# Gate and up projections of an expert pair, expert by expert instead of chunk by chunk, with one semaphore for each weight slot

## The reference, cut to what matters

```python
def expert_block(args):                    # for each expert e, over the tokens sent to it
    b_tok, b_w, e = args
    xb = xt[b_tok]
    h = jax.nn.silu(xb @ w_gate[e]) * (xb @ w_up[e])
    return (h @ w_down[e]) * b_w[:, None].astype(xt.dtype)
...
routed = jax.ops.segment_sum(y_rows.reshape(rows, d), row_tok, num_segments=t)
shared = (jax.nn.silu(xt @ sw_gate) * (xt @ sw_up)) @ sw_down
return (routed + shared).reshape(bsz, s, d)
```

## Time and profile before

| | |
|---|---|
| median of 3 runs | 1241.08 us |
| the profiled execution | 1241.98 us |
| its span (first to last instruction) | 1240.2 us |
| PE busy | 1183.7 us (95%), 7261 MATMUL records |
| PE weight loads busy | 546.2 us (44%) |
| DVE busy | 489.9 us (40%) |
| ACT busy | 193.6 us (16%) |
| read from HBM | 456.51 MB, 373 GB/s over the span |
| mean granted TensorE clock | 0.992 |

### The profile page before, as it was taken

The page is one execution under the profiler, slowest core; times in us unless marked ns, Lnnn a source line. Parts: engine busy times, 40 slices in busy tenths (PEclk is TensorE's granted clock), DMA queues, the critical chain, the costliest instruction groups (busy, mean ns, idle before and its releaser), DMA issues.

```text
span 1240.2 us, 17629 instructions
## 1 busy us (share of the span) xinstructions
PE 1183.7 (95%) x7261; PEld 546.2 (44%) x7261; DVE 489.9 (40%) x1059; ACT 193.6 (16%) x330; POOL 47.2 (4%) x78
## 2 busy tenths in 40 slices
PE   9999999999999999988899999999999999998886
PEld 8774833333333333332386757333333333333322
DVE  5895733332323332322237157333333232332224
ACT  3231311111111111110122313111111111111102
POOL 6300100000000000000010001000000000000000
PEclk9999999999999999999989999999999999999998
DMA  9788799999999999999953596999999999999995
GB/s 348 211 300 360 297 383 412 414 422 420 421 421 422 421 421 421 421 421 420 402 190 126 202 382 248 392 414 407 421 421 420 420 422 420 422 421 421 420 420 215
DMA packets 83642, 463.98 MB, mean 374 GB/s; under 512 B 9264, under 2 KB 10608, under 8 KB 38384
## 3 DMA queue, kind: packets, MB, share of 16 engines
q1 hardware_dynamic: 83424, 462.37, 92.2%
q10 hardware_dynamic: 144, 0.52, 0.1%
HBM read 456.51 MB, written 6.36 MB: 373 GB/s over the span
## 4 chain that ended last, share of the span: by engine, by line
PE 72%; DMA 22%; DVE 2%; SPq 1%; ACT 1%; issue 1%; DVEq 0%; POOL 0%; POOLq 0%
PE bank L1216 30%; DMA expert_weights<-in_exp_w_up 21%; PE bank L1272 12%; PE bank L724 5%; PE bank L738 4%; PE bank L1136 4%; PE bank L1166 3%; PE bank L812 2%; PE bank L1154 2%; DMA weight_ring<-in_sh_w_up 1%; PE bank L839 1%; PE bank L1085 1%; PE bank L828 1%; PE bank L1159 1%; PE bank L1232 1%; SPq L316 1%
## 5 line engine op out<-in xcount | busy, mean ns | idle before, releaser
L1216 PE MATMUL bank<-expert_weights,weight_ring 128*64 128x512 f32 x1024 | 226.8, 595 | 12.3 <-DMA expert_weights<-in_exp_w_up 12.3
L1272 PE MATMUL bank<-expert_weights,hiddenT 128*32 128x512 f32 x1888 | 218.4, 595 | 7.8 <-DVE hiddenT L2097 3.6
L2094 DVE TENSOR_TENSOR hidden<-silu_gate,bank 128x256 f32<-128x256 f32 x64 | 26.9, 421 | 391.7 <-ACT silu_gate L1492 391.7
L1216 PEld LDWEIGHTS bank<-expert_weights,weight_ring 128*64 128x64 f32 x1024 | 70.6, 137 | 166.6 <-issue 139.7
L1216 PE MATMUL bank<-expert_weights,hT 128*64 128x512 f32 x512 | 118.6, 606 | 17.2 <-DMA expert_weights<-in_exp_w_up 17.2
L1272 PEld LDWEIGHTS bank<-expert_weights,hiddenT 128*32 128x32 f32 x1888 | 56.4, 109 | 159.3 <-issue 138.9
L1216 PE MATMUL bank<-expert_weights,octet_high 128*64 128x512 f32 x512 | 115.3, 592 | 0.0
L2106 DVE TENSOR_SCALAR y_top<-bank,slot_gate 128x512 fp32r<-128x512 f32 x64 | 48.0, 750 | 126.2 <-PE bank L1272 126.2
L1492 ACT ACTIVATE silu_gate<-bank 128x256 f32<-128x256 f32 x64 | 24.7, 386 | 438.4 <-PE bank L1216 438.4
L1496 ACT ACTIVATE y_top<-bank,slot_gate 128x512 fp32r<-128x512 f32 x64 | 44.0, 687 | 286.4 <-PE bank L1272 286.4
L1216 PEld LDWEIGHTS bank<-expert_weights,hT 128*64 128x64 f32 x512 | 34.3, 138 | 101.4 <-issue 64.5
(11 more groups left out here) (388 smaller groups left out, 1114.2 us busy)
## 6 DMA issues: line engine op xcount, KB each, us to landing
expert_weights<-in_exp_w_down SPq DMA_DIRECT2D x114, 1024.0 KB, 17.2
expert_weights<-in_exp_w_gate SPq DMA_DIRECT2D x108, 1024.0 KB, 14.2
expert_weights<-in_exp_w_up SPq DMA_DIRECT2D x108, 1024.0 KB, 16.3
expert_weights<-in_exp_w_gate SPq DMA_DIRECT2D x40, 512.0 KB, 9.1
expert_weights<-in_exp_w_up SPq DMA_DIRECT2D x40, 512.0 KB, 10.9
weight_ring<-in_w_in_even SPq DMA_DIRECT2D x5, 2048.0 KB, 11.6
spare_down<-in_exp_w_down SPq DMA_DIRECT2D x10, 1024.0 KB, 11.8
weight_ring<-in_w_out SPq DMA_DIRECT2D x4, 2048.0 KB, 7.8
```

Of the source, the lines that this page charges most:

```text
L1216: last_mm = nc.tensor.matmul(bank[6][a * 2 * CAP:(a + 1) * 2 * CAP, :].rearrange("p (w f) -> p w f", w=2), octet_tokens(l, v, c)[:, 2 * q ...
L1272: last_mm = nc.tensor.matmul(bank[b][by_tile:by_tile + CAP, :], hm[:, j, own:own + CAP], down[a][:, j, half * 512:(half + 1) * 512], start ...
L2094: nc.vector.tensor_tensor(hslot[:, :], sg[:, :], bank[6][:, DE:2 * DE], ALU.mult)\
```

## The change

PE: the loop over the expert `a` becomes the outer one and the loop over the chunks `c` the inner one, so all 8 chunks of expert 0 come first, then all 8 of expert 1. Before each expert PE waits on a semaphore of that slot alone (`gu_in[2u+a]`, two loads). After expert 0 it raises a new semaphore `gu_first`. The waits and increments in the middle of a pair are gone. In the very first pair, the waits for each chunk of gathered tokens stand in expert 0's loop alone.

SP: gate and up of slot 2u are refilled on `gu_first`, those of slot 2u+1 on `gu_full`. `expert_chunks` and the loads by halves are gone; every load of gate and up is a whole one of 1 MB. The order of the down loads and of the spare buffers stays, and so do the halves of the last down loads. `early_refills` writes out the same sequence for the first pairs.

```diff
--- before.py
+++ after.py
@@ -204,11 +204,9 @@
                   "bt ct stored c_in b_in direct gla_ln gla_last decays masked hstat hstd yhead states y_s5 "
                   "gelu5 out_full")
         for l in range(2):
-            for name in ("gu_in", "d_in"):
-                MO[l][name] = [sem(f"moe{l}_{name}{u}") for u in range(2)]
-            MO[l]["second_part"] = sem(f"moe{l}_second_part")
-            MO[l]["last_part"] = sem(f"moe{l}_last_part")
-            MO[l]["gu_part"] = sem(f"moe{l}_gu_part")
+            MO[l]["gu_in"] = [sem(f"moe{l}_gu_in{s}") for s in range(NSLOT)]
+            MO[l]["d_in"] = [sem(f"moe{l}_d_in{u}") for u in range(2)]
+            MO[l]["gu_first"] = sem(f"moe{l}_gu_first")
             MO[l]["spare_in"] = sem(f"moe{l}_spare_in")
         ring_in = [sem(f"ring_in{i}") for i in range(2)]
 
@@ -313,16 +311,8 @@
         def expert_load(sp, m, l, e, s):
             src_g = A["exp_w_gate"][l, e].rearrange("(p c) f -> p (c f)", c=KC)
             src_u = A["exp_w_up"][l, e].rearrange("(p c) f -> p (c f)", c=KC)
-            sp.dma_start(ew[:, s, 0:EW], src_g).then_inc(m["gu_in"][s // 2], 16)
-            sp.dma_start(ew[:, s, EW:2 * EW], src_u).then_inc(m["gu_in"][s // 2], 16)
-
-        def expert_chunks(sp, l, e, s, chunks, landed):
-
-            lo, hi = chunks[0] * DE, (chunks[-1] + 1) * DE
-            src_g = A["exp_w_gate"][l, e].rearrange("(p c) f -> p (c f)", c=KC)
-            src_u = A["exp_w_up"][l, e].rearrange("(p c) f -> p (c f)", c=KC)
-            sp.dma_start(ew[:, s, lo:hi], src_g[:, lo:hi]).then_inc(landed, 16)
-            sp.dma_start(ew[:, s, EW + lo:EW + hi], src_u[:, lo:hi]).then_inc(landed, 16)
+            sp.dma_start(ew[:, s, 0:EW], src_g).then_inc(m["gu_in"][s], 16)
+            sp.dma_start(ew[:, s, EW:2 * EW], src_u).then_inc(m["gu_in"][s], 16)
 
         def down_half(sp, l, e, s, part, landed):
 
@@ -410,7 +400,6 @@
         def spare_load(sp, m, a, src):
             sp.dma_start(spare_d[a][:, :, :].rearrange("p j n -> p (j n)"), src).then_inc(m["spare_in"], 16)
 
-        BY_HALVES = (2, 3, 4, 5)
         LATE_SLOTS = ((2, 3), (3,))
         LN_INPUT = {"mix0": M0["out_full"], "mix1": M1["out_full"], "moe0": MO[0]["acc_full"], "moe1": MO[1]["acc_full"]}
         LAST_PARTS = ((0, 0, D), (1, 0, 512), (1, 512, D))
@@ -437,57 +426,53 @@
             spare_load(sp, m, 1, down_src(l, 5))
             sp.dma_start(ew[:, 3, 2 * EW:3 * EW], down_src(l, 7)).then_inc(m["d_in"][1], 16)
 
-            def refill(base, it, u, down=None):
-
-                sp.wait_ge(m["gu_full"], (base - 1) * 2 + u + 1)
-                for s in (2 * u, 2 * u + 1):
+            def refill_gu(base, it, u):
+
+                for s, read in ((2 * u, "gu_first"), (2 * u + 1, "gu_full")):
+                    sp.wait_ge(m[read], (base - 1) * 2 + u + 1)
                     expert_load(sp, m, l, it * NSLOT + s, s)
+
+            def refill_d(base, u, experts):
+
                 sp.wait_ge(m["y_hi_full"], (base - 1) * 2 + u + 1)
-                for s in (2 * u, 2 * u + 1):
-                    e = down[s - 2 * u] if down else it * NSLOT + s
+                for s, e in experts:
                     sp.dma_start(ew[:, s, 2 * EW:3 * EW], down_src(l, e)).then_inc(m["d_in"][u], 16)
 
-            def early_refill(ps, pair):
-
-                u = pair % 2
-                first = 2 * pair - 2 * u
-                later = m["last_part" if u else "second_part"]
-                if pair in BY_HALVES:
-                    sp.wait_ge(m["gu_part"], len(BY_HALVES) * ps + BY_HALVES.index(pair) + 1)
-                    for s in (2 * u, 2 * u + 1):
-                        expert_chunks(sp, l, first + s, s, range(0, 4), m["gu_in"][u])
-                sp.wait_ge(m["gu_full"], ps * PAIRS + pair - 1)
-                for s in (2 * u, 2 * u + 1):
-                    if pair in BY_HALVES:
-                        expert_chunks(sp, l, first + s, s, range(4, KC), later)
-                    else:
-                        expert_load(sp, m, l, first + s, s)
-                if pair == 6:
-                    return
-                sp.wait_ge(m["y_hi_full"], ps * PAIRS + pair - 1)
-                if pair == 4:
-                    for a in range(2):
-                        spare_load(sp, m, a, down_src(l, 12 + a))
-                    return
-                for s in (2,) if pair == 3 else (2 * u, 2 * u + 1):
-                    e = first + s + (NSLOT if pair == 2 else 0)
-                    sp.dma_start(ew[:, s, 2 * EW:3 * EW], down_src(l, e)).then_inc(m["d_in"][u], 16)
+            def refill(base, it, u):
+
+                refill_gu(base, it, u)
+                refill_d(base, u, [(s, it * NSLOT + s) for s in (2 * u, 2 * u + 1)])
+
+            def early_refills(ps):
+
+                base = ps * (NE // NSLOT) + 1
+                refill_gu(base, 1, 0)
+                refill_d(base, 0, ((0, 8), (1, 9)))
+                refill_gu(base, 1, 1)
+                refill_d(base, 1, ((2, 6),))
+                base = ps * (NE // NSLOT) + 2
+                refill_gu(base, 2, 0)
+                sp.wait_ge(m["y_hi_full"], (base - 1) * 2 + 1)
+                for a in range(2):
+                    spare_load(sp, m, a, down_src(l, 12 + a))
+                refill_gu(base, 2, 1)
+                refill_d(base, 1, ((2, 10), (3, 11)))
+                base = ps * (NE // NSLOT) + 3
+                refill_gu(base, 3, 0)
+                refill(base, 3, 1)
 
             def last_refill(ps):
 
-                sp.wait_ge(m["gu_full"], ps * PAIRS + PAIRS - 2)
-                for chunks, landed in ((range(0, 4), m["gu_in"][1]), (range(4, KC), m["last_part"])):
-                    for s in (2, 3):
-                        expert_chunks(sp, l, NE - NSLOT + s, s, chunks, landed)
-                sp.wait_ge(m["y_hi_full"], ps * PAIRS + PAIRS - 2)
+                base = ps * (NE // NSLOT) + NE // NSLOT - 1
+                refill_gu(base, NE // NSLOT - 1, 1)
+                sp.wait_ge(m["y_hi_full"], (base - 1) * 2 + 2)
                 for part, landed in enumerate((m["d_in"][1], m["spare_in"])):
                     for s in (2, 3):
                         down_half(sp, l, NE - NSLOT + s, s, part, landed)
 
             def refills(ps):
 
-                for pair in range(2, OCT):
-                    early_refill(ps, pair)
+                early_refills(ps)
                 with sp.Fori(OCT // 2, NE // NSLOT - 1) as it:
                     for u in range(2):
                         refill(ps * (NE // NSLOT) + it, it, u)
@@ -500,7 +485,8 @@
             with sp.If(npass > 1):
                 with sp.Fori(1, npass) as ps:
                     refill(ps * (NE // NSLOT), 0, 0)
-                    refill(ps * (NE // NSLOT), 0, 1, down=(2, 7))
+                    refill_gu(ps * (NE // NSLOT), 0, 1)
+                    refill_d(ps * (NE // NSLOT), 1, ((2, 2), (3, 7)))
                     spare_load(sp, m, 2, down_src(l, 3))
                     for a in range(2):
                         spare_load(sp, m, a, down_src(l, 4 + a))
@@ -1203,22 +1189,17 @@
                         elif q == 0:
                             pe.wait_ge(m["xg_lo"], n + 4)
                             pe.wait_ge(m["xg_hi"], n + 4)
-                        pe.wait_ge(m["gu_in"][u], 64 * g + 64)
-                        for c in range(KC):
-                            if opening:
-                                pe.wait_ge(m["xg_hi" if c % 2 else "xg_lo"], n + c // 2 + 1)
-                            if c == KC // 2 and first and k in BY_HALVES:
-                                pe.wait_ge(m["last_part" if u else "second_part"],
-                                           (192 if u else 128) * ps + (64 if k < OCT // 2 else 128))
-                            if c == KC // 2 and ending and q == 3:
-                                pe.wait_ge(m["last_part"], 192 * ps + 192)
-                            for a in range(2):
+                        for a in range(2):
+                            pe.wait_ge(m["gu_in"][2 * u + a], 32 * g + 32)
+                            for c in range(KC):
+                                if opening and a == 0:
+                                    pe.wait_ge(m["xg_hi" if c % 2 else "xg_lo"], n + c // 2 + 1)
                                 last_mm = nc.tensor.matmul(
                                     bank[6][a * 2 * CAP:(a + 1) * 2 * CAP, :].rearrange("p (w f) -> p w f", w=2),
                                     octet_tokens(l, v, c)[:, 2 * q + a, :, :].rearrange("p t s -> p (t s)"),
                                     ew_gu(2 * u + a, c), start=(c == 0), stop=(c == KC - 1))
-                            if first and k + 2 in BY_HALVES and c == KC // 2 - 1:
-                                last_mm.then_inc(m["gu_part"], 1)
+                            if a == 0:
+                                last_mm.then_inc(m["gu_first"], 1)
                         last_mm.then_inc(m["gu_full"], 1)
 
```

## The result

The kernel after has a median of 1542.54 us over 4 runs (1542.45 to 1543.45), against 1240.61 us for the kernel before in the same comparison. The ratio is 1.2424, with a 95% interval of 1.2404 to 1.2443: 302 us slower. The forecast was 1540 us.

What follows compares the result with a forecast made beforehand. PE and the loads were taken as nearly matched bounds, PE without spare time. 64 pairs x 5.15 = 329.6 us, less 31.2, gives +298.4 on 1242.0: 1540 us against the median of the runs, range 1500 to 1655 us.

Steps and rivals of the forecast that it cites:

- PE's own pace before, loads nearly matched, 31.2 us to win back: Pairs before: PE alone 13.43 us, loads 14.9 us; load waits and lower clock total 31.2 us, all of which goes away.
- Matmuls on the same columns go one at a time: Gate and up: records on the same array columns cannot run beside each other; 0.429 us a step.
- Three waiting records are passed, four steps shared, 28 steps: Gate and up: expert 1's first record starts with expert 0's 13th; a pair takes 28 steps instead of 16.
- The price of a pair: Gate and up of each pair: 12 x 0.429 = 5.15 us more, 12.2 us instead of 7.09.
- Periods: Pair to pair: 18.6 us in the first pairs, at most 20.1 us later, with loads at 310 to 340 GB/s.
- The new wait at nothing: The wait between the experts, on expert 1's first weight load, costs nothing; if it hinders passing, up to 1.7 us a pair.
- The loads' part hidden: Refills and whole loads: 3.7 to 5 us of air in every pair, so whole loads instead of halves cost nothing.
- Nothing passed: Rival at the mid-pair wait: PE finishes expert 0 first, 6.86 us more a pair, 1650 us; chance 0.15.
- more passed: Rival in gate and up: more waiting records passed than in L1047, 8 shared steps, 1431 us; chance 0.07.
- No cost: Rival: expert 1's records start beside expert 0's from the beginning; 1211 to 1242 us, likeliest 1240; chance 0.04.

Runs made afterwards that it cites:

- e1: The kernel after with the matmul order of the kernel before (experts alternating at every chunk), semaphores by slot and whole loads kept: 1246.45 us, ratio 1.0038.
- e2: The kernel before with its semaphores and loads by halves, but expert by expert on PE: 1541.35 us, ratio 1.2416.
- e10: The kernel after with each gate and up matmul split into one for gate and one for up, 256 moving columns each; sums differ from reference: 1602.25 us, ratio 1.2882.
- e5: The kernel before with the loops of down turned, both chunks of one 32-column group before the next group: 1243.20 us, ratio 1.0011.
- e6: The kernel after with the waits for both slots ahead of a pair's first matmul: 1541.85 us, ratio 1.2421.
- e3: The kernel after with the experts alternating in runs of 4 chunks: 1329.31 us, ratio 1.0706.
- e9: The kernel after with the experts alternating in runs of 3 chunks (3, 3, 2 of each): 1266.52 us, ratio 1.0183.

## Why the prediction was right

- *PE's own pace before, loads nearly matched, 31.2 us to win back.* Right in size: 64 x 5.20 = 332.8 us of added work made the span 1540.6 - 1240.2 = 300.4 us longer, so 32.4 us came back. After the change no wait of L1197 for a load is left. In moe0 pair 30, which had taken 8.78 us at the lower clock, takes 12.29 us like all others. One reading was weaker than it looked. Pair 19, taken for the pace of the loads, lies in the third group, where PE also has L1140 (L1154 before) to do. After the change PE waits for no load there:

```profile
518.97 12.29 PE L1197 MATMUL bank<-expert_weights,weight_ring 128*64 128x512 f32 x32
...
533.64 1.88 PE L1140 MATMUL bank<-h_low,gate_low_rankT 128*128 128x512 f32 x2
...
539.02 2.36 PE L1197 MATMUL bank<-expert_weights,hT 128*64 128x512 f32 x5
```

The period is 539.02 - 518.97 = 20.05 us, and without the added 5.20 it is 14.85: in this group PE alone sets nearly the 14.89 us of pair 19. The loads held PE back mainly in pairs 12 to 15 and 24 to 30 of a layer: from pair 24 on PE's own period is 18.63 - 5.20 = 13.43 us, and the kernel before took 14.9.
- *Matmuls on the same columns go one at a time.* Right, by order alone: e1 takes the order away and the loss goes, e2 brings the order alone and the loss comes, e10 rules out the place in the bank.
- *Three waiting records are passed, four steps shared, 28 steps.* Right in the trace of after (12 single starts, 4 double ones, 12 single), and by the runs of 2, 3 and 4 chunks. What I left open is that the count holds for each group of columns (e5).
- *The price of a pair.* 12 x 0.429 = 5.15 us was forecast and 12.29 - 7.09 = 5.20 us measured; the 0.05 is expert 1's first step. A group's first record is followed by the second after 0.48 us and not 0.43. Before, both experts take that step together, once a pair; after, expert 1 takes it again, as the next starts after 161.12 show:

```profile
155.40:155.90 0.50, 0.45 (x2) 1.00 1.08 459
155.40:155.95 0.55, 0.50 (x4) 1.00 1.06 447
...
155.90:161.57 5.67, 5.66 (x15) 1.00 0.86 351
155.90:161.62 5.72, 5.71 (x16) 1.00 0.85 349
```

(The first two are of the kernel before, the other two of the kernel after.) Over 64 pairs this is 3.2 us too little in the forecast. The waits gave back 1.2 us more than its 31.2, so that the two misses in part cancel.
- *Periods.* 18.6 us in the first group (measured 18.63) and at most 20.1 us later (measured up to 20.09, in the third group); 310 to 340 GB/s (315 and 320 in the windows shown).
- *The new wait at nothing.* Right (e6).
- *The loads' part hidden.* Right in the kernel after. By itself, next to the old order, it is a small loss: 5 us (e1), most of it because the last pair of a layer now waits for whole loads.
- *Rivals.* Nothing passed (1650 us) and more passed (1431 us) fell with the counted starts, and the argument for the latter, that longer records give PE time to get ahead, with e10, where steps half as long gave the same three. No cost (1240 us) is near what e1 shows for the loads alone, but its 1246.45 us lie above the 1211 to 1242 us given there: the loads were put at no loss, and cost 5 us when PE runs at the old pace.

The Trainium skill's sentence that tiles work independently ("TensorEngine Tiling (Array Packing)", Tiling Modes) holds in these runs as long as the program order brings work for the other columns soon enough. The depth of 64 of its page "TensorE: Matmul & The Clock Gate" ("Architectural detail") stands beside a partial reorder window that pulls weight loads ahead of running matmuls; the prediction's rival of no cost read it as a window over matmuls, which is not what that section says. The traces show no such depth for matmuls: with 16 records in a row the other columns got work only beside the 13th.

## What to carry to other kernels

Where matmuls use a part of the array's columns, the order in which they are issued decides whether the parts work beside each other: read the starts of the records, not their lengths, since 595 ns stayed 595 ns while the work took 73% longer. Change the group of columns at least every four records of one group, here every two f32 matmuls (1246.69 us, against 1246.45 with a change at every one); with six records in a row 20 us were lost. A finer wait for loads can win no more than what the engine waits for them, which should be summed before it is bought with the order of the work.

## What the runs showed of the hardware that was not expected

- The waiting records that PE passes are counted for each group of columns: with four groups, nine waited while the first record of the fourth started (e5). So it is three at least for these groups of 32 columns, and exactly three for the groups of 64 (after, e3, e9). It is the same with steps of 0.216 us as with 0.429 (e10).
- A wait that is not yet met holds up all that stands behind it: in e1 PE stood idle for 1.33 us with records of expert 0 behind the wait for expert 1's loads. A wait that is met does not keep later records from being passed ahead (after and e6, both 12.29 us).
- The half loads of a layer's last pair are worth more than its waits suggested: with whole loads each last pair got a wait in its middle, 4.6 us in all (e1), while PE had shown no wait at these pairs before.
